# Output and branch steps of the second tile's mixers in two parts each, with two slots of the expert sum behind each part

## The chip, the cores and the metric

One Trainium2 chip, one of its NeuronCores. The program is one launch. The metric is the device time of the launch in microseconds (us); lower is better. The engines are TensorE (PE), VectorE (DVE), ScalarE (ACT), GpSimd (POOL) and SyncE (SP); each works through its own list of instructions in order and waits for the others by semaphores. SP and POOL issue the transfers (DMA) from the chip's memory.

## The reference, cut to what matters

256 tokens of width 1024 in float32 go through two blocks. The first block has two mixers (a gated delta rule, and the HGRN2 recurrence), a mix of the two branches, and a retrieval of experts; the second block has pooling, attention and two feed-forward layers. The change lies in the first block:

```
o_b = _hgrn2_recurrence(...)            # chunks of 64 tokens: o = q S + a v ;  S = S * f + k v
y_a = o_a @ w_branch_a ; y_b = o_b @ w_branch_b
mix = sigmoid(g_a) * y_a + sigmoid(g_b) * y_b
x = x + mix @ w_out
h2 = rmsnorm(x) ; idx, gate = two top-16 searches over (h2 @ w_pq) and sub_keys
x = x + sum over 128 chosen experts of gate * gelu(h2 . expert_u[idx]) * expert_v[idx]
```

## The kernel before

The tokens are two tiles of 128. Each tile goes through the mixers (`delta0`, `hgrn0` for the first tile, `delta1`, `hgrn1` for the second), then through its tile steps (`tile0`, `tile1`), and then through the sum over its 128 chosen experts. The sum of the first tile is spread over the mixers and tile steps of the second tile, whose results it doesn't need.

**One slot of the expert sum.** A slot `r` (0 to 127 for the first tile, 128 to 255 for the second) is one expert for each of 128 tokens: one indirect transfer by POOL (line 888) gathers 128 rows of 8 KB, so 1 MB. DVE makes the dot product of half of each row with `h2` (line 906, with `accum_out`). ACT turns the dots of two slots (an even and the following odd one) into weights (lines 941, 944) and, except where `r` is a multiple of 4, writes the weight as a diagonal matrix (line 953). PE multiplies that diagonal with the other half of the row, into a sum in PSUM (line 972, two halves of 512 columns, which the trace shows as four rows per slot). Every fourth slot is added by DVE instead (line 919). The sum or add of slot `r` stands three slots behind its dot (`BEHIND = 3`): where the order table says that the slots up to `r` are worked on, PE sums slots up to `r - 3`.

**Buffers and gathers.** `Experts.place` decides beforehand which of 17 buffers a slot gets. POOL issues the gathers strictly in the order of the slots, and each waits until the slot that used the buffer before has been summed or added. Slot 71 takes the buffer of slot 63, slot 142 that of slot 128. From slot 72 on (`PARTS_FROM = 72`) the gathers wait for `hgrn_done(1)`, the last instruction of the second tile's HGRN mixer (line 793), because two of the buffers are its inputs. Four buffers are the places of the streamed weight panels, free for gathers only for slots 12 to 55 and from 128 on.

**Weight panels.** Weights stream in panels of 2 MB through two places; SP issues a panel when PE has finished the product that used its place (`stream`, line 360). The panels of the second tile are two for each of `branch_a`, `branch_b` and `w_out`, and four for `w_pq`. The product of a tile with one panel is 8 matmuls of 512 columns (`product_of_tile`, line 469).

**The order table.** `mixers_order` writes one list of entries `(program, stop)`. Each engine has one generator for each program, and `walk` runs the list on each engine: it advances the named generator up to the named `yield`. Entries made by `rows(n)` advance the expert sum by `n` slots. So an entry that has no instruction of an engine costs that engine nothing, and the table alone decides what stands before what in an engine's list.

The steps of `hgrn1` that the change touches, for each chunk `ch` of 64 tokens: PE makes the output `o.ch` (8 pairs of matmuls, lines 1484 and 1485) and the new part of the state `s.ch` (line 1443); DVE scales the state (line 1424, after `o.ch`) and adds `s.ch` (line 1426); ACT copies `o.ch` out (line 1362). `o.1` reads the state that DVE has made from `s.0`. After both chunks the gated norm follows (lines 774 to 793), whose last instruction is `hgrn_done`.

The steps of `tile1`: `turn_a`, `turn_b` turn the two mixers' outputs; `a`, `b` are the products with `branch_a` and `branch_b` (DVE multiplies each half by its gate, line 1696); `mix` adds and turns; `out` is the product with `w_out` (DVE adds to x, line 1709); `norm` makes `h2` and turns it; then the projections (`pq`), the scores (line 1590) and the searches `top`, `best`, `name` of five groups, nearly all of it DVE work.

## Time and profile before

| | us |
|---|---|
| median of 3 runs | 2010.41 (2004.6 to 2016.08) |
| the profiled execution, own time | 2016.91 |
| its span, first to last instruction | 2015.1 |

| engine | busy us | share |
|---|---|---|
| PE | 1728.3 | 86% |
| DVE | 821.7 | 41% |
| ACT | 449.5 | 22% |
| POOL | 310.8 | 15% |

In the profile, a row of a timeline gives the start in us from the span's start, the length in us, engine, line, operation, what it writes and reads, how many instructions are merged in it, and in brackets how long the engine had been idle before and what released it. A row of the windows gives, for one stretch, the busy us of PE, PE's weight loads, DVE, ACT and POOL (with counts of instructions), then the granted clock of TensorE (1.00 is 2.4 GHz, 0.50 is 1.2 GHz), the busy share of the DMA engines, and GB/s. A row of the DMA view gives a queue's packets, megabytes and share; the queue `q0` carries the gathers of POOL, `q1` what SP issues.

### The profile page before, as it was taken

What the parts mean: (1) busy time and instruction counts of PE and PEld (TensorE: products, weight loads), DVE (VectorE), ACT (ScalarE), POOL (GpSimd) and SP (SyncE); (2) the same over time, 40 slices, a digit from 0 to 9 for tenths busy, and PEclk for the clock granted to TensorE, in tenths of its full rate; (3) what the DMA queues carried; (4) which work ended last, traced back from release to release, by engine and by line L of the source; (5) the groups of instructions that cost most, each with busy time, mean ns of one, the idle gap of its engine ahead of it and who ended that gap; (6) DMA issues with size and microseconds to landing.
All of it is one profiled execution on the core that took longest, in us unless ns stands there. A gap on an engine that the chain in (4) does not pass through costs nothing.

```text
span 2015.1 us, 17726 instructions
## 1 busy us (share of the span) xinstructions
PE 1728.3 (86%) x6952; PEld 1135.5 (56%) x6952; DVE 821.7 (41%) x1564; ACT 449.5 (22%) x990; POOL 310.8 (15%) x260
## 2 busy tenths in 40 slices
PE   7999988997898588788965875677999999799998
PEld 6857656773675355434622422226887476478853
DVE  2433124422267786535999766662000013410001
ACT  1142114221132344212333322222000012310000
POOL 0000000000002253223344554430000000000000
PEclk9999978998889788789987989889999999899999
DMA  6444211114368799699999999993444343153442
GB/s 228 153 167 167 84 42 42 53 73 177 146 237 343 306 373 422 272 425 423 419 421 382 421 421 422 422 422 153 167 167 149 143 177 137 42 188 134 159 167 105
DMA packets 55184, 471.14 MB, mean 234 GB/s; under 512 B 6592, under 2 KB 7744, under 8 KB 10432
## 3 DMA queue, kind: packets, MB, share of 16 engines
q0 software_dynamic: 36864, 268.45, 32.4%
q1 hardware_dynamic: 18240, 201.60, 26.7%
q8 instruction: 53, 0.87, 0.2%
q14 instruction: 27, 0.22, 0.0%
HBM read 468.98 MB, written 1.05 MB: 233 GB/s over the span
## 4 chain that ended last, share of the span: by engine, by line
PE 61%; DMA 15%; DVE 14%; ACT 4%; issue 3%; POOL 1%; POOLq 0%; DVEq 0%; SPq 0%; ACTq 0%
PE ps L2282 15%; DMA main<-in_expert_uv,main 8%; PE ps L2306 7%; PE ps L469 6%; PE ps L425 6%; DMA panels<-in_expert_uv,main 5%; PE ps L395 4%; PE ps L1211 4%; DVE main L906 4%; PE ps L972 3%; PE ps L2259 3%; PE ps L2263 2%; PE ps L1443 2%; DMA panels<-in_wall 2%; PE ps L465 2%
## 5 line engine op out<-in xcount | busy, mean ns | idle before, releaser
L888 POOL DMA_INDIRECT main<-in_expert_uv,main x200 | 242.1, 1211 | 949.1 <-DVE main L1777 556.8
L972 PE MATMUL ps<-main 128*128 128x512 f32 x596 | 305.6, 663 | 81.5 <-ACT main L953 79.0
L2282 PE MATMUL ps<-xT,panels 128*128 128x256 f32 x1408 | 304.5, 379 | 0.8 <-DMA panels<-in_wall 0.8
L2282 PEld LDWEIGHTS ps<-xT,panels 128*128 128x128 f32 x1408 | 267.3, 190 | 37.2 <-DMA panels<-in_wall 0.9
L906 DVE SCALAR_TENSOR_TENSOR main<-main 128x1024 f32<-128x1024 f32 x200 | 240.7, 1223 | 106.5 <-DMA main<-in_expert_uv,main 105.0
L972 PEld LDWEIGHTS ps<-main 128*128 128x128 f32 x596 | 121.5, 213 | 246.8 <-issue 133.5
L2306 PE MATMUL ps<-panels,main 128*128 128x512 f32 x352 | 151.9, 593 | 2.3 <-DMA panels<-in_wall 2.3
L2359 DVE TENSOR_TENSOR main<-main,ps 128x512 f32<-128x512 f32 x22 | 15.1, 688 | 288.4 <-PE ps L2282 250.4
L972 PE MATMUL ps<-panels,main 128*128 128x512 f32 x172 | 93.7, 691 | 45.2 <-ACT main L953 38.4
L941 ACT ACTIVATE main<-main 128x2 f32<-128x2 f32 x128 | 25.9, 203 | 440.3 <-DVE main L906 334.7
L425 PE MATMUL ps<-panels,xT 128*128 128x512 f32 x256 | 117.0, 611 | 1.4 <-DVE main L1193 1.4
L2306 PEld LDWEIGHTS ps<-panels,main 128*128 128x128 f32 x352 | 66.7, 190 | 86.4 <-issue 82.3
L1211 PEld LDWEIGHTS ps<-main 128*128 128x128 f32 (+1 forms) x704 | 86.4, 200 | 14.8 <-issue 10.3
L1211 PE MATMUL ps<-main 128*128 128x128 f32 (+1 forms) x704 | 88.6, 284 | 5.8 <-ACT main L1087 1.7
L972 PEld LDWEIGHTS ps<-panels,main 128*128 128x128 f32 x172 | 36.4, 223 | 98.1 <-issue 61.1
L469 PE MATMUL ps<-panels,main 128*128 128x512 f32 x192 | 87.6, 616 | 3.4 <-ACT main L527 2.3
L395 PE MATMUL ps<-xT,panels 128*128 128x256 f32 x384 | 85.3, 386 | 1.3 <-PEq L562 1.3
L425 PEld LDWEIGHTS ps<-panels,xT 128*128 128x128 f32 x256 | 48.9, 196 | 58.1 <-issue 56.4
L395 PEld LDWEIGHTS ps<-xT,panels 128*128 128x128 f32 x384 | 74.4, 194 | 12.1 <-issue 1.7
L888 POOL DMA_INDIRECT panels<-in_expert_uv,main x56 | 68.5, 1223 | 81.2 <-DVE xT L919 27.2
L1443 PE MATMUL ps<-main 128*128 128x128 f32 (+1 forms) x288 | 50.3, 346 | 35.5 <-DVE main L1402 32.0
L906 DVE SCALAR_TENSOR_TENSOR panels<-panels,main 128x1024 f32<-128x1024 f32 x56 | 67.7, 1224 | 28.1 <-DMA panels<-in_expert_uv,main 27.6
(270 smaller groups left out, 1913.2 us busy)
## 6 DMA issues: line engine op xcount, KB each, us to landing
panels<-in_wall SPq DMA_DIRECT2D x88, 2048.0 KB, 8.0
main<-in_rows SPq DMA_DIRECT2D x14, 512.0 KB, 6.8
main<-in_expert_uv,main POOLq DMA_INDIRECT x200, 18.1
main<-in_sub_keys SPq DMA_DIRECT2D x2, 1024.0 KB, 13.9
mats<-in_mats SPq DMA_DIRECT2D x1, 1088.0 KB, 5.4
x<-in_x SPq DMA_DIRECT2D x2, 512.0 KB, 3.9
main<-in_pool_w SPq DMA_DIRECT2D x1, 1024.0 KB, 33.6
main<-in_rel_bias SPq DMA_DIRECT2D x1, 1024.0 KB, 15.1
```

What stands on the lines that cost most here:

```text
L395: mm = pe.matmul(self.ps[:, bank, t * T:(t + 1) * T], w[:, k, c:c + P], actT[:, k, :], start=(k == 0), stop=(k == KC - 1))
L425: mm = pe.matmul(self.ps[:, bank, :], self.xT[:, k, j * P:(j + 1) * P], w[:, k, :], start=(k == 0), stop=(k == KC - 1))
L465: mm = pe.matmul(self.ps[:, bank, t * P:(t + 1) * P], w[:, k, t * P:(t + 1) * P], actT[:, k, :], start=(k == 0), stop=(k == KC - 1))
L469: mm = pe.matmul(self.ps[:, bank, :], actT[:, k, :], w[:, k, :], start=(k == 0), stop=(k == KC - 1))
L888: pool.indirect_dma_start(out=self.bufs[self.buf_of[r]], out_offset=None, in_=self.c.dram["expert_uv"], in_offset=bass.IndirectOffsetOnAxi ...
L906: dve.scalar_tensor_tensor(out=u, in0=u, scalar=1.0, in1=self.c.row(m, H2), op0=ALU.mult, op1=ALU.mult, accum_out=self.dots_at[:, m, q:q + ...
L972: mm = pe.matmul(self.c.ps[:, b, :], self.diags[self.of_pe(r) % DIAG_RING], v[:, half * HALF:(half + 1) * HALF], start=(q == 1), stop=(q = ...
L1211: mm = pe.matmul(out[:, h, :], lhs(h), rhs(h), start=True, stop=True)
L1443: mm = pe.matmul(out[:, h, :], lhs(h), rhs(h), start=True, stop=True)
L2259: mm = pe.matmul(c.ps[:, bank, t * T + m * P:t * T + (m + 1) * P], w[:, k, at:at + P], c.xT[:, k, m * P:(m + 1) * P], start=(k == 0), stop ...
L2282: mm = pe.matmul(c.ps[:, bank, t * T:(t + 1) * T], w[:, k, at:at + P], c.xT[:, k, :], start=(k == 0), stop=(k == KC - 1))
L2306: mm = pe.matmul(c.ps[:, 4 + 2 * m + half, :], hidden[:, n, m * P:(m + 1) * P], w[:, n % 4, half * HALF:(half + 1) * HALF], start=(n == 0) ...
```

## The change

Two kinds of entries of the table are cut in two. In `hgrn1` the new stop `seen{ch}` stands behind the matmuls of `o.ch` and before those of `s.ch` (on DVE and ACT it stands before everything of the chunk); two slots follow it, and two, then one, follow the stops `o{ch}` and `S{ch}`. In `tile1` the steps `a`, `b` and `out` have a stop behind the product with their first panel (`a0`, `b0`, `out0`), and two slots follow each of the seven stops. No instruction is added or taken away; the slots after both chunks stand at 72 where they stood at 70, and the two extra slots are taken back at the end of the first tile's sum, behind `best3`.

```diff
@@ hgrn_tensor
         mm.then_inc(un.filled(), 1)
+        yield f"seen{ch}"
         heads(f"s.{ch}", lambda h: t.k_dec[r, h, :], lambda h: t.v[r, h, :])
@@ tile_tensor
-    c.products_of_tile(pe, t.names[0], t.aT, channel_major=False)
+    c.product_of_tile(pe, t.names[0], 0, t.aT, channel_major=False)
+    yield "a0"
+    c.product_of_tile(pe, t.names[0], 1, t.aT, channel_major=False)
     yield "a"
@@ tile_vector
             dve.tensor_tensor(at, at, c.ps[:, bank, :], ALU.mult).then_inc(c.bank_read[bank].sem, 1)
+            if q == 0:
+                yield ("a0", "b0")[n]
@@ mixers_order
     for ch in range(2):
+        part("hgrn1", f"seen{ch}")
+        rows(2)
         part("hgrn1", f"o{ch}")
-        rows(3)
+        rows(2)
         part("hgrn1", f"S{ch}")
         rows(1)
...
-    part("tile1", "a")
-    rows(4)
...
-    part("tile1", "out")
-    rows(4)
+    for x in ("a0", "a", "b0", "b", "mix", "out0", "out"):
+        part("tile1", x)
+        rows(2)
     part("tile1", "norm")
     rows(3)
```

The same stops stand in the ACT programs and for `b0` and `out0`. How the lists of the engines move is seen best in the lists themselves. First PE, before, around the second chunk of `hgrn1`: L1443 x8 is `s.0` and later `s.1`, the pairs of L1484 and L1485 between are `o.1`, and L972 with x6 is the sum of three slots.

```order
L1443 MATMUL ps<-main 128x128 x8
L972 MATMUL ps<-main 128x512 x6
L1484 MATMUL ps<-main 128x128
L1485 MATMUL ps<-main 128x128
...
L1443 MATMUL ps<-main 128x128 x8
L972 MATMUL ps<-main 128x512 x10
L518 MATMUL ps<-mats,main 128x128 x8
```

The same place of the PE list in the changed kernel (its lines 1445, 1486 and 1487 are the same instructions):

```order
L972 MATMUL ps<-main 128x512 x2
L1445 MATMUL ps<-main 128x128 x8
L972 MATMUL ps<-main 128x512 x6
L1486 MATMUL ps<-main 128x128
L1487 MATMUL ps<-main 128x128
...
L972 MATMUL ps<-main 128x512 x2
L1445 MATMUL ps<-main 128x128 x8
L972 MATMUL ps<-main 128x512 x10
L518 MATMUL ps<-mats,main 128x128 x8
```

Slot 59 is now summed before `s.0`, slots 61, 62 and 63 before `o.1` (before: 59, 61, 62), and slot 65 between `o.1` and `s.1`.

Next DVE, before, from the first chunk's state (L1424, L1426) to the gated norm (L786); L906 is a dot, L919 an add:

```order
L906 SCALAR_TENSOR_TENSOR main<-main 128x1024
L1424 TENSOR_TENSOR main<-main 128x1024
L1426 TENSOR_TENSOR main<-main,ps 128x1024
L906 SCALAR_TENSOR_TENSOR main<-main 128x1024 x3
L919 SCALAR_TENSOR_TENSOR xT<-main,xT 128x8x128
L906 SCALAR_TENSOR_TENSOR main<-main 128x1024
L1424 TENSOR_TENSOR main<-main 128x1024
L1426 TENSOR_TENSOR main<-main,ps 128x1024
L906 SCALAR_TENSOR_TENSOR main<-main 128x1024
L786 TENSOR_REDUCE small<-main 128x8
```

And in the changed kernel, where L1426 and L1428 are the two state instructions:

```order
L906 SCALAR_TENSOR_TENSOR main<-main 128x1024 x2
L1426 TENSOR_TENSOR main<-main 128x1024
L1428 TENSOR_TENSOR main<-main,ps 128x1024
L906 SCALAR_TENSOR_TENSOR main<-main 128x1024 x2
L919 SCALAR_TENSOR_TENSOR xT<-main,xT 128x8x128
L906 SCALAR_TENSOR_TENSOR main<-main 128x1024 x3
L1426 TENSOR_TENSOR main<-main 128x1024
L1428 TENSOR_TENSOR main<-main,ps 128x1024
L906 SCALAR_TENSOR_TENSOR main<-main 128x1024
L919 SCALAR_TENSOR_TENSOR xT<-main,xT 128x8x128
L786 TENSOR_REDUCE small<-main 128x8
```

The dot of slot 65 now stands before the first state step, those of slots 69 and 70 before the second one, and the dot of slot 71 and the add of slot 68 before the norm.

Last PE again, the tile steps, before; L469 is a product, 8 for each panel, and L518 a turn:

```order
L469 MATMUL ps<-panels,main 128x512 x16
L972 MATMUL ps<-main 128x512 x6
L469 MATMUL ps<-panels,main 128x512 x16
L972 MATMUL ps<-main 128x512 x6
L518 MATMUL ps<-mats,main 128x128 x8
L972 MATMUL ps<-main 128x512 x4
L469 MATMUL ps<-panels,main 128x512 x16
```

and in the changed kernel:

```order
L469 MATMUL ps<-panels,main 128x512 x8
L972 MATMUL ps<-main 128x512 x2
L469 MATMUL ps<-panels,main 128x512 x8
L972 MATMUL ps<-main 128x512 x4
L469 MATMUL ps<-panels,main 128x512 x8
L972 MATMUL ps<-main 128x512 x2
L469 MATMUL ps<-panels,main 128x512 x8
L972 MATMUL ps<-main 128x512 x4
L518 MATMUL ps<-mats,main 128x128 x8
L972 MATMUL ps<-main 128x512 x2
L469 MATMUL ps<-panels,main 128x512 x8
```

The sums of one or two slots stand between the products with the two panels of each weight.

## Rows read from the trace of the kernel before

**Rows 1.** The page: span, and GB/s in 40 equal slices of 50.4 us.

```profile
span 2015.1 us, 17726 instructions
...
GB/s 228 153 167 167 84 42 42 53 73 177 146 237 343 306 373 422 272 425 423 419 421 382 421 421 422 422 422 153 167 167 149 143 177 137 42 188 134 159 167 105
```

**Rows 2.** Windows: busy us of each engine, clock, DMA share, GB/s.

```profile
core 0: us, PE busy (x) PEld busy (x) DVE busy (x) ACT busy (x) POOL busy (x), PEclk, DMA share, GB/s
855.00:1070.00 215.00, 165.15 (x576) 90.15 (x576) 153.62 (x417) 58.40 (x163) 73.87 (x63) 0.89 1.01 422
1070.00:1085.00 15.00, 10.84 (x19) 4.70 (x20) 14.90 (x26) 5.88 (x19) 6.14 (x5) 0.68 0.83 311
1085.00:1366.00 281.00, 196.91 (x398) 79.61 (x396) 184.56 (x277) 78.70 (x277) 139.51 (x109) 0.90 1.00 416
...
828.00:845.00 17.00, 17.00 (x51) 10.43 (x51) 9.40 (x11) 5.83 (x9) 1.21 (x2) 0.73 0.18 65
```

**Rows 3.** Timeline of POOL: the gathers of slots 71, 72 and 142.

```profile
837.99 0.94 POOL L888 DMA_INDIRECT main<-in_expert_uv,main  x1 [17.82 <-PE ps L972]
844.73 1.68 POOL L888 DMA_INDIRECT main<-in_expert_uv,main  x1 [5.80 <-DVE main L793]
...
1074.72 1.68 POOL L888 DMA_INDIRECT panels<-in_expert_uv,main  x1 [13.83 <-DVE xT L916]
```

**Rows 4.** Timeline of PE, 800 to 845 us.

```profile
800.99 0.46 PE L1484 MATMUL ps<-main 128*128 128x128 f32 x2
...
807.53 1.95 PE L1443 MATMUL ps<-main 64*128 64x128 f32 x16
...
815.48 2.60 PE L972 MATMUL ps<-main 128*128 128x512 f32 x4 [2.36 <-ACT main L953]
819.33 0.80 PE L1484 MATMUL ps<-main 128*128 128x128 f32 x2 [1.26 <-DVE main L1426]
...
830.77 3.62 PE L1443 MATMUL ps<-main 64*128 64x128 f32 x16
834.32 10.26 PE L972 MATMUL ps<-main 128*128 128x512 f32 x20
```

**Rows 5.** Timeline of DVE, 813 to 845 us: dots of slots 63 and 67, state, norm.

```profile
813.14 1.23 DVE L906 SCALAR_TENSOR_TENSOR main<-main 128x1024 f32<-128x1024 f32 x1 [5.54 <-DMA main<-in_expert_uv,main]
...
818.05 1.22 DVE L1426 TENSOR_TENSOR main<-main,ps 128x1024 f32<-128x1024 f32 x1
...
823.07 1.23 DVE L906 SCALAR_TENSOR_TENSOR main<-main 128x1024 f32<-128x1024 f32 x1 [1.22 <-DMA main<-in_expert_uv,main]
...
839.15 1.22 DVE L786 TENSOR_REDUCE small<-main 128x8 f32<-128x1024 f32 x1 [2.16 <-ACT main L774]
...
843.23 1.22 DVE L793 TENSOR_TENSOR main<-main,small 128x1024 f32<-128x1024 f32 x1
```

**Rows 6.** Timeline of PE from the start of the `branch_a` product.

```profile
873.61 13.97 PE L469 MATMUL ps<-panels,main 128*128 128x512 f32 x32 [1.56 <-ACT main L527]
887.42 5.31 PE L972 MATMUL ps<-main 128*128 128x512 f32 x12
```

**Rows 7.** Timeline of DVE: slots 79, 99, first search, slots 111 and 128.

```profile
870.41 1.22 DVE L906 SCALAR_TENSOR_TENSOR main<-main 128x1024 f32<-128x1024 f32 x1 [1.25 <-DMA main<-in_expert_uv,main]
...
951.94 1.23 DVE L906 SCALAR_TENSOR_TENSOR main<-main 128x1024 f32<-128x1024 f32 x1 [1.25 <-DMA main<-in_expert_uv,main]
...
960.22 0.48 DVE L1726 MAX8 main<-main 128x8 f32<-128x128 f32 x2
...
995.23 1.22 DVE L906 SCALAR_TENSOR_TENSOR main<-main 128x1024 f32<-128x1024 f32 x1
...
1069.12 1.22 DVE L906 SCALAR_TENSOR_TENSOR panels<-panels,main 128x1024 f32<-128x1024 f32 x1
```

**Rows 8.** DMA queues, 0 to 951.9 us: packets, MB, share.

```profile
q0 software_dynamic: 14498, 105.66, 27.4%
```

**Rows 9.** DMA queues, 0 to 1000 us: packets, MB, share.

```profile
q0 software_dynamic: 16514, 120.32, 29.7%
```

More of the change, by code:

```diff
@@ L1421, in hgrn_vector @@
         last = CHUNK * (ch + 1) - 1
+        yield f"seen{ch}"
         yield f"o{ch}"
@@ L1486, in hgrn_tensor @@
         mm.then_inc(un.filled(), 1)
+        yield f"seen{ch}"
         heads(f"s.{ch}", lambda h: t.k_dec[r, h, :], lambda h: t.v[r, h, :])
@@ L1545, in tile_tensor @@
         pe.wait_ge(c.bank_read[b].sem, n)
-    c.products_of_tile(pe, t.names[1], t.bT, channel_major=False)
+    c.product_of_tile(pe, t.names[1], 0, t.bT, channel_major=False)
+    yield "b0"
+    c.product_of_tile(pe, t.names[1], 1, t.bT, channel_major=False)
     c.uses_at[f"mix.{m}"] = list(c.bank_uses)
@@ L1552, in tile_tensor @@
     wait_turned_tile_read(c, pe)
-    c.products_of_tile(pe, t.names[2], t.mixT, channel_major=False)
+    c.product_of_tile(pe, t.names[2], 0, t.mixT, channel_major=False)
+    yield "out0"
+    c.product_of_tile(pe, t.names[2], 1, t.mixT, channel_major=False)
     c.uses_at[f"out.{m}"] = list(c.bank_uses)
@@ L1624, in tile_scalar @@
     read_turned_tile(c, act, t.bT, 4 * m + 1)
-    yield "a"
-    yield "b"
+    for stop in ("a0", "a", "b0", "b"):
+        yield stop
     read_turned_tile(c, act, t.mixT, 4 * m + 2)
-    yield "mix"
-    yield "out"
+    for stop in ("mix", "out0", "out"):
+        yield stop
     for b in (0, 2):
@@ L1709, in tile_vector @@
         dve.tensor_tensor(at, at, c.ps[:, bank, :], ALU.add).then_inc(c.bank_read[bank].sem, 1)
+        if q == 0:
+            yield "out0"
     yield "out"
@@ L1967, in mixers_order @@
     rows(4)
-    part("tile1", "a")
-    rows(4)
-    part("tile1", "b")
-    rows(4)
-    part("tile1", "mix")
-    rows(2)
-    part("tile1", "out")
-    rows(4)
+    for x in ("a0", "a", "b0", "b", "mix", "out0", "out"):
+        part("tile1", x)
+        rows(2)
     part("tile1", "norm")
```

## The prediction, on record before the changed kernel ran

> **What bounds the kernel now.** I first read the page's row of GB/s [rows 1]: from slice 12 to slice 26 (605 to 1360 us) the gathers fill the memory path at about 422 GB/s, with holes in slices 13, 14, 16 and 21. The change acts from 807 us on, so only the holes of slices 16 and 21 are in question. The windows cut them out [rows 2]: from 828 to 845 us the DMA share is 0.18, which is 14 us lost; from 855 to 1070 it is 1.01, nothing lost; from 1070 to 1085 it is 0.83, 2.6 us lost; from 1085 to 1366 it is 1.00. What follows after 1366 doesn't depend on the order in question. So the time moves by what the gathers' stream moves: when it resumes near 845, and how long it runs dry near 1075.
>
> The timeline of POOL names the gates [rows 3]. Slot 71's gather waited 17.8 us for a sum on PE and went out at 837.99: it needs slot 63's buffer, and that sum stood behind `o.1` and `s.1`. Slot 72's waited for line 793, `hgrn_done(1)`, and went out at 844.73. Slot 142's went out at 1074.72, after the first DVE instruction for slot 128 (line 916), which stands behind the last search of `tile1`. In 855 to 1070 DVE is the other full engine: from the first search at 960.22 to slot 128's dot at 1069.12 [rows 7] it has next to no idle time.
>
> **The first hole, piece by piece.** In the changed kernel slot 63's sum stands before `o.1`, so slot 71's gather leaves at about 821 instead of 837.99. That is the full 17 us that the move seems to promise, but it buys one gather: slot 72 and all behind it still wait for `hgrn_done(1)`. So I follow that chain, from the rows of PE and DVE [rows 4, 5].
>
> - Up to 813 nothing arrives earlier: slot 63's dot starts at 813.14 when its row lands, and its weight lets PE sum slots 62 and 63 from 815.48. The first takes 2.60 us as now, the second 1.8 to 3.5. PE is free at 820 to 821.6.
> - DVE now makes slot 65's dot before the first state step. Rows land about every 2.5 us here (1 MB at 422 GB/s), slot 67's at 823.07, so slot 65's at 818.1. The dot (1.2) and two state instructions (2.45) give 821.8. Now the state is ready at 819.27 (818.05 + 1.22). **`o.1` starts at 821.9, 2.6 us later than now.**
> - `o.1` took 11.4 us (819.33 to 830.77), while `o.0`, the same 8 pairs of matmuls, took 6.5 (800.99 to 807.53). The granted clock explains it: 1.2 GHz for the one, 2.4 for the other. PE had idled 2.36 and 1.26 us just before the slow one. In the change two 512-column sums stand together right before `o.1`, with about 1 us of idle time left. The row at 834.32 shows what such sums do: five slots took 10.26 us, near the 1.77 for a slot at full clock [rows 6], so the clock had come back under them after `s.1`. I take the full clock for `o.1`, and keep the other.
> - With the full clock: `o.1` ends 828.4, slot 65's sum 830.2, `s.1` 832.1. DVE meanwhile waits for rows: slots 69 and 70 land at 828.0 and 830.5, the dot of 70 ends at 831.7, two state instructions end at 834.2. Slot 71's row has landed (833), its dot ends 835.4, the add of slot 68 836.6; ACT's weight and square put the norm's reduction at 837.7. From there to the end of line 793 it is 5.3 us (839.15 to 844.45): 843.0. **The resume moves by -1.5 us.** It can't be much better whatever PE does: slots 70 and 71 have to land first.
> - With the half clock: `o.1` ends 833.3, the sum by 836.8, `s.1` at 838.7 to 840.4; state, dot, add, weight and square add 5 us, the norm 5.3: 849.0 to 850.7, **+4.5 to +6.2**.
>
> **The tile steps.** Two more slots stand before `a`. PE started it at 873.61, released by ACT, which had waited for slot 79's dot at 870.41 [rows 6, 7]. Now it is slot 81's, two rows later: the products start 5.0 us later against the stream. From there on the counts are alike: 14 slots up to `norm` before and after, on PE 10 sums where there were 11. The interleaving lets ACT weigh one pair less before the turned mix can be read, and two dots less stand before the square of x; each saves 1 to 3 us of waiting, and three sums instead of two before the projections give 1.8 back. So the path from `a` to the first search, 86.6 us now (873.61 to 960.22), gets back most of the 5.0 us. The rows themselves are there: slot 99's dot ran at 951.94 as soon as its row landed, slot 101's runs two rows later, at 956.9, and ends at 958.1. I let the search start 1 to 2 us earlier than now, and that matters little, as the next part shows: what is late on PE here is covered by the wait for rows there, up to some 6 us. The last panel loads of `w_pq` and what SP issues behind them start about 5 us later too.
>
> **The second hole.** From the first search on DVE has the same work less two dots: 28 slots up to 128 before, 26 after, 2 x 1.2 = 2.4 us. But it asks for rows two numbers higher at the same place, with no stock: slot 99 was still waited for at 951.94. The queue view says when a row is there [rows 8, 9]: at 951.9 us 105.66 MB had come for slots 0 to 99 (104.86 MB), so 0.8 MB lies in rows behind; slot 113 (114 rows, 119.54 MB) is in when 120.34 MB have come, at 1000.0 us. DVE took slot 111 at 995.23 before, and would take slot 113 at that place, by its own work at about 993.3. So it waits for the stream. The loads of SP that came in between (`w_pq`, then the pooling constants) begin about 5 us later and leave the gathers a little more of the path; I take 1.0 us from it. Slot 113's dot then ends at 1000.2. Slot 111's ended at 996.4 and slot 128's began 72.7 us later; less 2.4 that is 70.3, so 1070.5, **+1.4 us** against 1069.12 (0 to +2.8 by how SP's loads fall). As the stream runs dry there now, slot 142's gather, and everything behind, moves by it. If DVE were not starved, the hole would close: -2.6 us, no more, since the share is 1.0 on both sides.
>
> **A rule that speaks against it.** The granted clock in 828 to 845 is 0.73 with PE busy throughout [rows 2, 4]. The Trainium skill, "TensorE: Matmul & The Clock Gate", section "A second HAM failure mode: psum-queue depth-cycling", says that short idle gaps between groups of matmuls can make the clock swing and that the groups then pay for it. By that rule finer pieces on PE hold the clock down; this trace agrees in so far as short gaps stood before the slow `o.1`. Its result here is the first rival below.
>
> **Sum.** -1.5 + 1.4 = -0.1 us against the profiled execution's 2016.9, which lies 6.5 above the median of the runs shown; I take the difference over to the median: 2010.3.
>
> **The rivals.**
> 1. *The forecast*: full clock in `o.1`, DVE starved a little: -0.1 (-1.5 to +1.3). Chance 0.50.
> 2. *Slower: the clock stays at 1.2 GHz* through `o.1`, slot 65's sum and `s.1`, as now through `o.1`. For it: the gaps before `o.1` shrink but don't go. Against it: the sums just ahead. 4.5 + 1.4 = +5.9, up to 6.2 + 2.8 = +9.0, so 2016.3 to 2019.4. It passes the bound of 0.5% (10 us) only where `hgrn_done` comes 8.5 us later than 844.45 or the runs' own spread adds to it. Chance 0.25.
> 3. *Both edits pay*: resume -1.5 and the hole near 1075 gone, -4.1, so 2006.3. For it: DVE has 2.4 us less to do and starts searching earlier. Against it: the byte count above. Chance 0.18.
> 4. *The 14 us hole closes*, -10 or more. The wait on line 793 excludes it unless the norm comes much earlier, and the landing of slot 71 excludes that. Chance 0.03. The rest, 0.04, is for panels of `branch_b` landing later beside a deeper queue of gathers (12.3 us are free for each, a panel product and three sums [rows 6]).
>
> The runs of the kernel before spread from 2004.6 to 2016.1, so a difference under 0.5% is about what a measurement of this kernel can't tell from none. The range takes cases 1 to 3 and a little of that spread: 2003 to 2020. Faster by over 0.5%: 0.03 and a part of case 3, 0.07. Slower by over 0.5%: a part of case 2 and the panels, 0.13. Within: 0.80.
>
> **What the profile of the changed kernel would show.** Slot 71's gather within 2 us of slot 70's, and the long idle time of POOL before the gather of slot 72, still released by line 793, at 843 (or 849 to 851 if rival 2 is right). The windows still with a hole of some 12 to 18 us before it. The second run of lines 1486 and 1487 in 6.5 us at clock 1.0, starting near 822. `branch_a`'s product near 877, with sums between its panels and no wait for panels. DVE waiting for gathers at slots 105 to 113, which it doesn't now, and a hole near 1075 of 2 to 6 us. The prediction is wrong if the gather of slot 72 is released by something else, if DVE never waits in its searches, or if the part after 1366 changes in length.

## The result, and the profile after

The changed kernel took 2015.26 us in the median of 20 runs (2007.41 to 2023.78), the kernel before 2007.15 us in 20 runs beside it (2001.69 to 2016.08). The ratio is 1.0035 with an interval of 1.002 to 1.005: slower by 7 us (4 to 10), where -0.1 was forecast. The profiled execution of the changed kernel took 2013.05 us.

The two profiled executions already differ by 8 us ahead of slot 63's dot (it starts at 813.14 before [rows 5], at 805.18 after), in a part whose code is the same. So from here on times within the stretch count from **the start of slot 63's dot**, written t+. First the page and the windows of the changed kernel, to be laid beside [rows 1, 2]:

```profile
span 2011.3 us, 17726 instructions
...
GB/s 228 155 165 170 84 42 43 64 63 178 146 274 344 281 401 423 268 423 424 419 421 386 421 421 422 422 415 132 172 163 155 138 181 133 42 189 135 158 167 105
```

```profile
core 0: us, PE busy (x) PEld busy (x) DVE busy (x) ACT busy (x) POOL busy (x), PEclk, DMA share, GB/s
821.00:839.00 18.00, 17.66 (x56) 9.21 (x55) 11.28 (x15) 7.09 (x14) 0.00 (x0) 0.84 0.14 56
855.00:1070.00 215.00, 164.13 (x575) 89.04 (x574) 155.96 (x422) 59.95 (x167) 70.67 (x60) 0.87 1.01 418
1070.00:1085.00 15.00, 14.57 (x31) 5.86 (x31) 14.90 (x22) 5.42 (x21) 10.00 (x9) 0.92 0.88 353
1085.00:1366.00 281.00, 194.51 (x393) 78.38 (x392) 183.11 (x273) 77.76 (x273) 134.93 (x106) 0.89 0.98 408
```

Slice 16 still has its hole (268 GB/s, before 272), and the first window has a share of 0.14 over 18 us: 15.5 us lost, where it was 14. POOL's timeline, beside [rows 3], says why:

```profile
812.49 0.94 POOL L888 DMA_INDIRECT main<-in_expert_uv,main  x1 [0.30 <-issue]
839.50 0.94 POOL L888 DMA_INDIRECT main<-in_expert_uv,main  x1 [26.07 <-DVE main L793]
...
1070.23 1.68 POOL L888 DMA_INDIRECT panels<-in_expert_uv,main  x1 [22.11 <-DVE xT L916]
```

Slot 71's gather goes out at once after slot 70's (t+7.3, before t+24.9). Slot 72's waits for line 793 as before, and goes out at t+34.3 instead of t+31.6. Slot 142's is at t+265.1 instead of t+261.6. PE in the second chunk of `hgrn1`, beside [rows 4]:

```profile
807.51 3.70 PE L972 MATMUL ps<-main 128*128 128x512 f32 x8 [1.69 <-ACT main L953]
813.81 0.49 PE L1486 MATMUL ps<-main 128*128 128x128 f32 x2 [2.60 <-DVE main L1428]
...
815.90 0.48 PE L1487 MATMUL ps<-main 64*128 64x128 f32 x2
816.31 0.68 PE L1486 MATMUL ps<-main 128*128 128x128 f32 x2
816.92 0.79 PE L1487 MATMUL ps<-main 64*128 64x128 f32 x2
...
823.43 3.60 PE L972 MATMUL ps<-main 128*128 128x512 f32 x4
826.96 2.05 PE L1445 MATMUL ps<-main 64*128 64x128 f32 x16
```

`o.1` begins at full clock (0.49 us for two matmuls). From 816.9 on the same two take 0.79: the granted clock has fallen to 1.2 GHz. It stays there through slot 65's sum (3.60 us for what takes 1.8 to 2 at full clock) and is back at `s.1`. PE had stood idle for 1.69 and 2.60 us just before. The norm, beside [rows 5], ends 2.8 us later against slot 63 than it did (t+34.1 against t+31.3):

```profile
829.11 1.22 DVE L1428 TENSOR_TENSOR main<-main,ps 128x1024 f32<-128x1024 f32 x1 [4.18 <-PE ps L1445]
...
833.92 1.22 DVE L786 TENSOR_REDUCE small<-main 128x8 f32<-128x1024 f32 x1 [1.12 <-ACT main L774]
...
838.00 1.23 DVE L793 TENSOR_TENSOR main<-main,small 128x1024 f32<-128x1024 f32 x1
```

And DVE further on, the waits that stand beside [rows 7]:

```profile
921.53 0.69 DVE L1720 TENSOR_TENSOR x<-x,ps 128x512 f32<-128x512 f32 x1 [5.91 <-PE ps L469]
...
931.83 0.69 DVE L1720 TENSOR_TENSOR x<-x,ps 128x512 f32<-128x512 f32 x1 [7.32 <-PE ps L469]
...
954.64 0.49 DVE L1739 MAX8 main<-main 128x8 f32<-128x128 f32 x2 [1.74 <-ACT main L1664]
961.01 1.28 DVE L919 SCALAR_TENSOR_TENSOR xT<-main,xT 128x1024 f32<-128x1024 f32 x1 [0.65 <-ACT main L944]
986.46 1.23 DVE L906 SCALAR_TENSOR_TENSOR main<-main 128x1024 f32<-128x1024 f32 x1 [2.48 <-DMA main<-in_expert_uv,main]
```

The products start at t+68.0 (PE's first matmul with `branch_a`), before at t+60.5. DVE waits 5.91 and 7.32 us for the two halves of the `w_out` product. The kernel before has this pair of waits too:

```profile
923.22 0.69 DVE L1709 TENSOR_TENSOR x<-x,ps 128x512 f32<-128x512 f32 x1 [6.50 <-PE ps L469]
930.09 0.69 DVE L1709 TENSOR_TENSOR x<-x,ps 128x512 f32<-128x512 f32 x1 [6.18 <-PE ps L469]
```

The first search starts at t+149.5, before at t+147.1. Slot 111's dot waits 2.48 us for its row in the midst of the searches, where nothing waited before. From slot 142's gather to slot 255's it is 264.5 us; before it is 265.7. So in the profiles the stream behind slot 142 is shifted, not stretched, and what is to be explained lies ahead of it.

### The profile page after: what moved, and what is told of

The parts are those of the page before. It is cut to its first block, busy times and chain, and to the rows that moved or that the text cites. A ratio compares the mean times of both kernels' runs of the same rounds, so it can differ in the third digit from the quotient of the medians.

```text
span 2011.3 us, 17726 instructions
## 1 busy us (share of the span) xinstructions
PE 1715.6 (85%) x6952; PEld 1122.6 (56%) x6952; DVE 822.1 (41%) x1564; ACT 449.4 (22%) x990; POOL 309.4 (15%) x260
## 4 chain that ended last, share of the span: by engine, by line
PE 61%; DMA 16%; DVE 13%; ACT 4%; issue 3%; POOL 2%; POOLq 0%; DVEq 0%; SPq 0%; ACTq 0%
PE ps L2292 15%; DMA main<-in_expert_uv,main 10%; PE ps L2316 7%; PE ps L469 6%; PE ps L425 6%; DMA panels<-in_expert_uv,main 5%; PE ps L395 4%; PE ps L1211 4%; PE ps L972 4%; DVE main L906 3%; PE ps L2269 3%; PE ps L2273 2%; PE ps L1445 2%; PE ps L465 2%; DMA panels<-in_wall 2%
## 5 line engine op out<-in xcount | busy, mean ns | idle before, releaser
L972 PE MATMUL ps<-main 128*128 128x512 f32 x596 | 309.3, 667 | 89.4 <-ACT main L953 88.9
L906 DVE SCALAR_TENSOR_TENSOR main<-main 128x1024 f32<-128x1024 f32 x200 | 241.0, 1222 | 114.6 <-DMA main<-in_expert_uv,main 110.5
L972 PEld LDWEIGHTS ps<-main 128*128 128x128 f32 x596 | 121.4, 214 | 256.0 <-issue 135.2
L972 PE MATMUL ps<-panels,main 128*128 128x512 f32 x172 | 90.2, 669 | 52.9 <-ACT main L953 46.2
L972 PEld LDWEIGHTS ps<-panels,main 128*128 128x128 f32 x172 | 35.0, 214 | 103.9 <-issue 69.2
L469 PE MATMUL ps<-panels,main 128*128 128x512 f32 x192 | 87.9, 615 | 4.5 <-ACT main L527 3.2
L906 DVE SCALAR_TENSOR_TENSOR panels<-panels,main 128x1024 f32<-128x1024 f32 x56 | 67.6, 1222 | 28.1 <-DMA panels<-in_expert_uv,main 25.1
```

The source lines that it names most:

```text
L469: mm = pe.matmul(self.ps[:, bank, :], actT[:, k, :], w[:, k, :], start=(k == 0), stop=(k == KC - 1))
L906: dve.scalar_tensor_tensor(out=u, in0=u, scalar=1.0, in1=self.c.row(m, H2), op0=ALU.mult, op1=ALU.mult, accum_out=self.dots_at[:, m, q:q + ...
L972: mm = pe.matmul(self.c.ps[:, b, :], self.diags[self.of_pe(r) % DIAG_RING], v[:, half * HALF:(half + 1) * HALF], start=(q == 1), stop=(q = ...
```

## The experiments

Each was timed in five rounds beside the kernel before, 12 runs in all (6 for e15, 7 for e17); the first two rows have the times of the section above. "hd" is the end of the last line 793 (`hgrn_done`), "g" a gather's issue, "d" a dot's start. All of these are read from one profiled execution of each and counted from slot 63's dot. The length of `o.1` is taken from the start of its first row to that of its last. "Slots" says how many slots stand before the tile's products and before the first search.

| kernel | slots | ratio, interval | o.1, us | hd | g72 | products | d128 | g142 |
|---|---|---|---|---|---|---|---|---|
| before | 80/100 | 1 | 10.8 | 31.3 | 31.6 | 60.5 | 256.0 | 261.6 |
| changed | 82/102 | 1.0035, 1.002 to 1.005 | 8.9 | 34.1 | 34.3 | 68.0 | 259.5 | 265.1 |
| e1 | 82/102 | 1.0016, 0.9999 to 1.0033 | 9.5 | 36.6 | 36.9 | 71.3 | 265.2 | 270.8 |
| e2 | 80/100 | 0.999, 0.9974 to 1.0006 | 10.9 | 31.3 | 31.5 | 60.5 | 256.4 | 262.0 |
| e3 | 80/100 | 1.0003, 0.9985 to 1.002 | 10.1 | 32.9 | 33.1 | 61.6 | 258.8 | 264.4 |
| e4 | 80/100 | 0.9959, 0.994 to 0.9977 | 9.4 | 30.5 | 25.6 | 55.1 | 251.6 | 257.2 |
| e5 | 82/102 | 1.002, 0.9995 to 1.0045 | 6.2 | 30.9 | 31.2 | 65.9 | 259.4 | 265.0 |
| e6 | 80/100 | 1.0008, 0.9984 to 1.0031 | 9.8 | 33.1 | 33.3 | 62.1 | 259.6 | 265.1 |
| e7 | 82/102 | 0.9976, 0.9952 to 1.0 | 6.2 | 30.0 | 12.6 | 50.9 | 245.1 | 250.7 |
| e8 | 80/100 | 0.9983, 0.9958 to 1.0009 | 10.8 | 27.9 | 28.2 | 57.0 | 252.6 | 258.2 |
| e9 | 82/100 | 1.003, 1.0007 to 1.0052 | 6.1 | 30.9 | 31.1 | 63.5 | 258.4 | 264.0 |
| e10 | 80/100 | 0.998, 0.9957 to 1.0004 | 9.6 | 30.0 | 30.3 | 58.4 | 243.6 | 253.5 |
| e11 | 82/102 | 0.9945, 0.9925 to 0.9964 | 10.9 | 37.6 | 13.7 | 59.0 | 241.3 | 251.2 |
| e12 | 80/100 | 0.9988, 0.997 to 1.0006 | 9.3 | 30.4 | 24.8 | 54.6 | 241.0 | 250.9 |
| e13 | 80/100 | 0.9987, 0.9972 to 1.0001 | 6.1 | 29.0 | 29.3 | 58.6 | 254.1 | 259.8 |
| e14 | 80/102 | 1.0034, 1.0014 to 1.0054 | 6.3 | 29.9 | 30.1 | 58.6 | 256.8 | 262.4 |
| e15 | 82/102 | 0.9933, 0.9914 to 0.9951 | 6.3 | 30.0 | 12.6 | 51.4 | 233.5 | 243.4 |
| e16 | 80/100 | 0.9998, 0.998 to 1.0015 | 6.1 | 25.2 | 25.5 | 53.9 | 249.5 | 255.1 |
| e17 | 80/100 | 0.9965, 0.9946 to 0.9984 | 6.2 | 28.5 | 17.9 | 50.4 | 237.5 | 247.4 |

**Which half of the change.** Both edits are made on the changed kernel: e1 gives it the tile steps of before, e2 the `hgrn1` steps of before.

```diff
-    for x in ("a0", "a", "b0", "b", "mix", "out0", "out"):
-        part("tile1", x)
-        rows(2)
+    part("tile1", "a")
+    rows(4)
+    part("tile1", "b")
+    rows(4)
+    part("tile1", "mix")
+    rows(2)
+    part("tile1", "out")
+    rows(4)
```

```diff
-        part("hgrn1", f"seen{ch}")
-        rows(2)
         part("hgrn1", f"o{ch}")
-        rows(2)
+        rows(3)
```

> Only the half of the change in hgrn1 (seen, o, S followed by 2, 2 and 1 slots per chunk); the tile steps keep 4, 4, 2 and 4 slots. Theory A (the loss is that hgrn_done, and with it the gather of slot 72, comes later): all of the loss is here, +4 to +8 us against before, ratio 1.002 to 1.004, and the gather of slot 72 comes 32 to 35 us after the dot of slot 63, where it came 31.6 us after it before. Theory B (the loss comes from the sums between the halves of the products and the wait for rows in the searches behind them): 0 to +1 us. The forecast on record: -0.1 us.

> Only the half of the change in tile1 (two slots behind each of a0, a, b0, b, mix, out0, out); hgrn1 keeps 3 and 1 slots per chunk. Theory A: 0 us or a little faster (-3 to +1), since the slots before the products stand where they stood and the path to the first search is 1 to 3 us shorter. Theory B: +4 to +8 us. The forecast on record would give -1 to -3 us, down to the 2.6 us of the second hole.

e2 can't be told from before in its time, and its columns lie within 0.5 us of it: parting the tile steps alone brings nothing. In its profile e1 has the whole shift and more: `o.1` mostly at half clock, `hgrn_done` 5.3 us later, slot 128 9.2 us later. Its time, 1.0016, is clear neither of before nor of the changed kernel. So it is the profiles that put the loss in the edit in `hgrn1`; the times show that the tile edit alone doesn't have it.

**The slots or the stops.** e3 is the changed kernel with one slot behind `o{ch}` instead of two, so that the counts are those of before:

```diff
         part("hgrn1", f"o{ch}")
-        rows(2)
+        rows(1)
```

> The whole change with one slot instead of two behind o0 and o1, so that 4 slots stand in each chunk as before, and slot 71 is no longer dotted before the norm. Theory A, if the loss is the work put before the norm (the wait for the row of one more slot, its dot, an add): hgrn_done comes 1 to 4 us earlier than in the full change and the ratio falls to 0.999 to 1.002. Theory A, if the loss is the granted clock in o.1 alone: no gain against the full change, 1.003. Theory B: 1.003 as well, as the tile steps keep their form.

Ratio 1.0003, with `hgrn_done` 1.6 us and slot 128 2.8 us later than before: between the two in the profile, and no loss in the time that can be measured.

**The price of a late gate.** e6 is the kernel before with four more DVE instructions, 5.00 us in its trace, ahead of the second tile's gated norm (they write a buffer that nothing reads any more); e8 is the kernel before with the four slots behind `o1`, `S1` all behind the gate step; e4 moves the gate itself, so that the gathers need the HGRN buffers only from slot 84 on, and e7 is the same on the changed kernel. The edits, in this order:

```diff
+    if m == 1:
+        for _ in range(4):
+            step(dve.tensor_tensor(t.k_t, t.k_t, t.k_t, ALU.mult))
```

```diff
-    for ch in range(2):
-        part("hgrn1", f"o{ch}")
-        rows(3)
-        part("hgrn1", f"S{ch}")
-        rows(1)
-    part("hgrn1", "gate")
+    part("hgrn1", "o0")
+    rows(3)
+    part("hgrn1", "S0")
+    rows(1)
+    part("hgrn1", "o1", "S1", "gate")
+    rows(4)
```

```diff
-PARTS_FROM = 72
+PARTS_FROM = 84
```

> The kernel before with four more DVE multiplications of 1.2 us, one after the other, before the reduction of hgrn1's norm (on a slot of memory that nobody reads any more). A dose for theory A: hgrn_done comes 4.9 us later, slot 72's gather 36.5 us after slot 63's dot instead of 31.6, and if the stream of gathers sets the end the time rises by 4 to 5 us, ratio 1.0020 to 1.0025; slot 142's gather moves by as much. If the later hole or DVE takes it up: 0 to 1 us.

> The kernel before with the four slots of the second chunk of hgrn1 moved behind the norm, so that o.1, s.1, the state and the norm follow each other without a dot between. Theory A: slot 72's gather is released earlier, by 1 to 3 us (one dot less and no weights before the square), but slot 71's may be later; ratio 0.998 to 1.000. If only the granted clock counts: 1.000.

> The kernel before with PARTS_FROM 84 instead of 72: the two buffers that lie in the inputs of the HGRN mixer take their first slot at 84, and no gather before slot 84 waits for hgrn_done. Theory A (the wait of slot 72 for hgrn_done opens the hole of 14 us, and the stream of gathers sets the end): the hole shrinks by 5 to 12 us and the time falls by 2.6 us to 12 us, as far as DVE follows (the second hole near 1075 takes the rest): ratio 0.994 to 0.999. Theory B: the end hangs on DVE's searches, and these on the products; the products start on slot 79's dot, so they start earlier too; 0.995 to 1.0. If the hole costs nothing: 1.000.

> The changed kernel with PARTS_FROM 84 instead of 72, so that no gather before slot 84 waits for hgrn_done. If the loss of the change is the later hgrn_done, it is gone here: the sums of slots 63 to 67 stand early, the gathers from 72 on leave 18 to 27 us after slot 63's dot, and the time is 5 to 12 us under before and at or under that of the same edit on the kernel before (0.9959): ratio 0.993 to 0.997. If the change costs time elsewhere (product stage, searches), it stays 3 to 6 us above that one: 0.998 to 1.0.

Slot 72's gather 3.4 us earlier (e8) brings slot 142's 3.4 earlier; 6.0 (e4) brings 4.4; 21.7, from the changed kernel to e7, brings 14.4. e6 was a weaker dose than meant: DVE had stood idle for 2.16 us ahead of the norm [rows 5], and `o.1` was 1.0 us shorter in that execution, so `hgrn_done` came only 1.8 later, yet slot 142's gather 3.5. So in these pairs two thirds or more of what slot 72's gather gains or loses is handed on to slot 142; e5 below is an exception. e4 is also clearly faster in time, and e7, with all of the change in it, has 0.9976 where the changed kernel has 1.0035. But e7's expectation missed: its time isn't under e4's 0.9959 (the intervals overlap), though its profile has slot 142's gather 6.5 us earlier. e7's POOL timeline around slot 72:

```profile
814.19 0.94 POOL L888 DMA_INDIRECT main<-in_expert_uv,main  x1 [0.99 <-PE ps L972]
818.82 1.82 POOL L888 DMA_INDIRECT main<-in_expert_uv,main  x1 [3.70 <-DVE xT L919]
823.76 1.85 POOL L888 DMA_INDIRECT main<-in_expert_uv,main  x1 [3.12 <-PE ps L972]
827.65 1.62 POOL L888 DMA_INDIRECT main<-in_expert_uv,main  x1 [2.04 <-PE ps L972]
```

Each gather waits a few us for a buffer, none for line 793. Slice 16 of its page is at 394 GB/s.

**The clock.** e5 is the changed kernel with three matmuls that nothing reads, put where PE waits for the state ahead of `o.1`:

```diff
+        if m == 1 and ch == 0:
+            for _ in range(3):
+                pe.matmul(c.ps[:, 0, :], c.mat("ident"), c.mats[:, 0:4, :].rearrange("p h n -> p (h n)"),
+                          start=True, stop=True)
```

> The changed kernel with three more matmuls on PE between slot 63's sum and the wait for the state before o.1 (a constant matrix into a bank that nothing reads; they write no result). They fill some 2.6 us in which PE waits for DVE anyway. Clock theory (the norm is late because TensorE's granted clock falls within o.1 after that wait): o.1 runs in about 6.5 us instead of 9.6, slot 72's gather comes 28 to 31 us after slot 63's dot instead of 34.3, and the time falls by 3 to 6 us against the changed kernel, ratio to before 0.998 to 1.001. Work theory (the dots and adds that stand before the norm make it late, whatever the clock): slot 72's gather stays at 33 to 35 us, ratio 1.002 to 1.004.

```profile
808.87 5.40 PE L972 MATMUL ps<-main 128*128 128x512 f32 x8 [1.99 <-ACT main L953]
814.10 2.74 PE L1495 MATMUL ps<-mats 128*128 128x512 f32 x6
...
822.83 0.48 PE L1487 MATMUL ps<-main 64*128 64x128 f32 x2
823.24 1.98 PE L972 MATMUL ps<-main 128*128 128x512 f32 x4
```

With the idle time filled, `o.1` takes 6.2 us at full clock to its last pair, slot 65's sum 1.98. `hgrn_done` comes 3.2 us earlier than in the changed kernel, though the filler itself makes `o.1` start 1.5 us later. The seven kernels with the filler all have 6.1 to 6.3 us; of the twelve without, e7 alone has. e1 and e7 have the same lists up to there, and rows that agree to 0.02 us: 5.40 us of sums, idle times of about 1.97 and 0.91 us. Yet in e1 (first three rows) the clock fell within `o.1`, and slot 65's sum took 3.78; in e7 (last three) it stayed and the sum took 1.98:

```profile
808.36 5.40 PE L972 MATMUL ps<-main 128*128 128x512 f32 x8 [1.96 <-ACT main L953]
814.67 0.49 PE L1486 MATMUL ps<-main 128*128 128x128 f32 x2 [0.91 <-DVE main L1428]
...
824.92 3.78 PE L972 MATMUL ps<-main 128*128 128x512 f32 x4
...
808.52 5.40 PE L972 MATMUL ps<-main 128*128 128x512 f32 x8 [1.98 <-ACT main L953]
814.84 0.49 PE L1486 MATMUL ps<-main 128*128 128x128 f32 x2 [0.92 <-DVE main L1428]
...
821.50 1.98 PE L972 MATMUL ps<-main 128*128 128x512 f32 x4
```

e11 has the same order up to there too and took 10.9 us at clock 0.50, where PE had been idle for 3.65 us just before. Its row, and then e7's window, 6.2 us at 1.00:

```profile
809.57 0.80 PE L1486 MATMUL ps<-main 128*128 128x128 f32 x2 [3.65 <-DVE main L1428]
```

```profile
814.80:821.00 6.20, 6.16 (x30) 4.44 (x30) 4.89 (x7) 1.27 (x5) 2.14 (x2) 1.00 1.02 422
```

So without the filler the clock there is a chance of the execution, and the idle time alone doesn't decide it. That the filler keeps it up, seven profiles of seven show; they show it in the profile alone, since e5's time (1.002) can't be told from the changed kernel's. But e5 moves slot 128 by 0.1 us alone: a second loss stands behind the first.

**The second loss.** Its candidates are the two slots more ahead of the products and the two more ahead of the first search. e9, e13 and e14 complete four corners around e5, all with the filler. In order e9, e13, e14, against e5:

```diff
     part("tile1", "norm")
-    rows(3)
+    rows(1)
```

```diff
         part("hgrn1", f"o{ch}")
-        rows(2)
+        rows(1)
```

```diff
     part("hgrn1", "gate")
-    rows(3)
+    rows(1)
...
     part("tile1", "norm")
-    rows(3)
+    rows(5)
```

> The changed kernel with the three filling matmuls before o.1, and with one slot instead of three behind tile1's norm, so that 100 slots stand before the first search, as before the change, and not 102. Two-cause theory (the change costs once through o.1 at a low clock, which the filling takes away, and once through two more rows that DVE asks for in its searches before the stream has them): slot 128's dot comes 255 to 257 us after slot 63's, where it came 256.0 before, 259.5 in the changed kernel and 259.4 with the filling alone, and the time is that of before, ratio 0.999 to 1.001. One-cause theory (only the late hgrn_done): no gain against the run with the filling alone, slot 128's dot at 259 to 260, ratio 1.002.

> The changed kernel with three identity matmuls of 512 columns ahead of the second tile's output chunk 1 (they write a row block that nothing reads any more, so that TensorE has no idle time before that chunk), and with one slot instead of two behind each of the two new output parts: 80 slots before the tile's products and 100 before the first search, as in the kernel before. Theory (the 3 us that stay when the clock is filled away come from the two slots that stand ahead of the products and the two that stand ahead of the search): slot 128's dot at 255.5 to 256.5 us after slot 63's (before: 256.0; with the filler and all slots: 259.4), slot 142's gather at 261 to 262, products at 59 to 61, ratio 0.998 to 1.001. Rival (the parts themselves, or the three fillers, cost it, whatever the slots): slot 128's dot again at 258.5 to 259.5, ratio 1.001 to 1.004.

> The same filler, one slot behind the gate step and five behind the norm step: 80 slots before the products, and 102 before the first search, as in the changed kernel. Theory A (the later products carry the loss): slot 128's dot at 255.5 to 257 us after slot 63's, products at 59 to 61, ratio 0.998 to 1.001. Theory B (the two slots more before the search carry it, since the searches then ask for rows two numbers higher while the gathers are no further on): slot 128's dot at 258.5 to 259.5 and DVE waiting for rows at slots 107 to 113, ratio 1.001 to 1.004. In between (257 to 258.5): each carries a part.

| d128 after slot 63's dot, ratio | 100 before the search | 102 |
|---|---|---|
| 80 before the products | 254.1, 0.9987 | 256.8, 1.0034 |
| 82 before the products | 258.4, 1.003 | 259.4, 1.002 |

In the profiles each step adds something: 4.3 and 2.6 us for the slots before the products, 2.7 and 1.0 for those before the search. But each is one profile, and the corners aren't clean. e5, e9 and e14 have the same lists up to `hgrn_done` and still lie 1.0 us apart there, and e13 ends it up to 1.9 us earlier, since it takes its slots out ahead of the norm. So the 1.0 isn't clear of the scatter, and of the 4.3 up to 1.9 is an earlier gate. In time e9 and e14 are slower than before; e13 isn't, and e5's interval takes in 1.

Where the second loss lies is seen at the start of the first search. In e5 the late products have been made good by then: it starts at t+146.0, before at t+147.1. The wait of 7.33 us for the second `w_out` product is no new loss, as the pair of waits there is 13.24 us, and 12.68 in the kernel before. From the first search to slot 128's dot it is 108.9 us before, 108.9 in e9 and 109.0 in e13, all with 100 slots ahead of it; with 102 and so two dots less to make, it is 110.0 in the changed kernel, 112.8 in e14 and 113.4 in e5. DVE's rows in e5:

```profile
920.79 0.69 DVE L1724 TENSOR_TENSOR x<-x,ps 128x512 f32<-128x512 f32 x1 [5.91 <-PE ps L469]
...
931.09 0.69 DVE L1724 TENSOR_TENSOR x<-x,ps 128x512 f32<-128x512 f32 x1 [7.33 <-PE ps L469]
...
983.45 1.22 DVE L906 SCALAR_TENSOR_TENSOR main<-main 128x1024 f32<-128x1024 f32 x1 [2.18 <-DMA main<-in_expert_uv,main]
987.72 1.22 DVE L906 SCALAR_TENSOR_TENSOR main<-main 128x1024 f32<-128x1024 f32 x1 [3.04 <-DMA main<-in_expert_uv,main]
```

So the second loss is the wait for rows in the searches: 0.49, 2.18 and 3.04 us at slots 107, 110 and 111, where before has none. In e9 these are gone, and this one stands ahead of the first search:

```profile
962.31 1.28 DVE L919 SCALAR_TENSOR_TENSOR xT<-main,xT 128x1024 f32<-128x1024 f32 x1 [8.52 <-ACT main L944]
```

The add needs a weight that ACT makes only after it has copied out the scores. The kernel before has that wait too (5.84 us); with 102 slots the weight is made earlier and 0.65 is left. So e9's expectation missed: taking back the two slots cures the rows and brings this wait back, longer by 2.7 us, and the search starts at t+149.5. e14 has row waits of 1.48 and 3.48 us in the searches, and e13 none there. e14's time (1.0034) is worse than its profile (+0.8 us at slot 142); one profile of each kernel can't settle that.

**The filler in the kernel before.** e16 adds the lines of e5 to the kernel before, and nothing else.

> The kernel before with the same three identity matmuls of 512 columns ahead of the second tile's output chunk 1, and nothing else: it has one order step less to wait through there, and its chunk 1 took 10.8 us at half the clock. Theory (the half clock in chunk 1 is a loss that the kernel before has as well, and the parts bring nothing of their own): chunk 1 in 6.1 to 6.5 us, the tile's last state write at 28 to 29.5 us after slot 63's dot (before: 31.3), slot 128's dot at 253 to 254.5 (before: 256.0; the changed kernel with four slots less in front and the filler, e13: 254.1), ratio 0.9975 to 1.0. Rival (e13's 254.1 is owed to the parts, and the filler only pays back what the parts cost): the last state write at 30 to 31.5, slot 128's dot at 255.5 to 257, ratio 0.999 to 1.002.

`o.1` takes 6.1 us, `hgrn_done` comes 6.1 us earlier and slot 142's gather 6.5, more than was expected. e13 has the same slot counts and the same filler, with the new stops besides: it ends `hgrn_done` 3.8 us behind e16 and starts slot 128's dot 4.6 us behind it. So at one and the same clock the change makes `hgrn_done` later by itself: 3.8 us in e13, 5.7 in e5. In its profile the kernel before paid for a slow `o.1`, and that had hidden this. Yet e16's time is 0.9998, so what the profile gains isn't seen in it. In this execution the tail from slot 255's dot to the end took 657.1 us, and 649.7 in that of before; over all the profiles it is 650 to 657, with the same code.

**A better version.** e10 gives the steps of the last search (group 4; two expectations call it the fourth) two slots each in the kernel before. The table had `rows(3)` there, nine slots by its text, but `most` is 128 and slot 128 had been reached ahead of this search, so no slot stood in it; now slots 128 to 133 do. Further, e11 puts that and the gate at 84 on the changed kernel, e12 on the kernel before; e15 adds the filler to e11, and e17 has e3's slot counts besides.

```diff
-        part("tile1", f"top{g}")
-        rows(3)
-        part("tile1", f"best{g}")
-        rows(3)
-        part("tile1", f"name{g}")
-        rows(3)
+        n, most = (2, SLOTS + 8) if g == 4 else (3, SLOTS)
+        for x in ("top", "best", "name"):
+            part("tile1", f"{x}{g}")
+            rows(n, most)
```

> The kernel before with two slots behind each step of the last search (top4, best4, name4) where it had none, and so slots 128 to 133 begun before the search is over. If the hole of 2.6 us near 1075 comes from slot 142's gather waiting for slot 128's first add, that gather leaves some 10 us earlier, the hole closes and the time falls by 2 to 3 us: ratio 0.9985 to 0.999. If the hole is opened by something else: 1.000.

> The changed kernel with both holes attacked: PARTS_FROM 84, and two slots behind each step of the last search. The stream of gathers should have less than 3 us of idle time from slot 63 to slot 255. Against before (14 us and 2.6 us of holes, one gather of 2.5 us in them) that is -13 to -17 us in the stream: ratio 0.992 to 0.995. If DVE is the bound of that stretch instead, slot 255's dot gains no more than with PARTS_FROM 84 alone (11 us), ratio 0.996 to 0.998.

> The same two edits on the kernel before (PARTS_FROM 84, and two slots behind each step of the last search), so without the change. Against the run with both edits on the changed kernel it shows what the change is worth once slot 72 no longer waits for the norm: there slots 63 and 65 are summed ahead of s.1, here the stream waits for them behind o.1 and s.1 (7 to 9 us of idle time in the first hole). Expected ratio 0.994 to 0.997; if the change costs time in the tile steps, this one is the faster of the two.

> The changed kernel with the parts' products from slot 84 instead of 72, the fourth search's steps on six slots instead of nine, and the filler. Theory (the clock lost in output chunk 1 is the delay of the gated gather that e11 kept): output chunk 1 in 6.2 us instead of 10.9, the second tile's last state write at 30 to 31 us after slot 63's dot instead of 37.6, slot 142's gather at 245 to 249 instead of 251.2, slot 255's at 514 to 517 instead of 519.4, ratio 0.990 to 0.994. Rival (the stream's bytes to slot 142 and the fourth search decide, not the gate): slot 142's gather stays at 250 to 252, ratio 0.9935 to 0.996.

> e15 (parts' products from slot 84, the fourth search's steps on six slots, the filler) with one slot instead of two behind each output part, so 80 slots before the products and 100 before the first search. Theory (the two slots in front cost 2 to 5 us at slot 128 in the kernels with a gated gather at 72, as e13 against e5 and e14 shows): slot 142's gather 2 to 4 us earlier than e15's 243.4, ratio 0.990 to 0.993. Rival (with the gate moved to slot 84 the rows are far enough ahead that the searches don't starve DVE): slot 142's gather at 242.5 to 244.5, ratio 0.992 to 0.995, the same as e15 (0.9933 [0.9914, 0.9951]).

e15 is the fastest: 1996.37 us against 2008.26, ratio 0.9933 (0.9914 to 0.9951). It had 6 runs. Its windows, with both holes all but closed:

```profile
801.00:856.00 55.00, 45.13 (x146) 22.87 (x144) 39.84 (x55) 17.53 (x50) 23.16 (x21) 0.94 0.99 405
1036.00:1051.00 15.00, 4.93 (x7) 1.80 (x8) 14.62 (x53) 5.15 (x12) 1.03 (x2) 0.61 0.92 380
```

Beside e11 the profile has 7.8 us less at slot 142, the time only 0.9933 against 0.9945, which their intervals don't part. e12 against e11 went the other way than their profiles: slot 142's gather at 250.9 and 251.2, but ratios 0.9988 and 0.9945. That stays open, and e12 missed its expectation (0.994 to 0.997). e10 brings slot 142's gather 8.1 us forward, but slot 255's only 3.6 (t+523.7 against t+527.3), and its interval takes in 1. e17's theory fell, and slot 142's gather came even later than its rival had it: in this pair of profiles the two slots in front no longer cost; without them DVE waits 6.94 us for the same add as in e9, and the gather is 4.0 us later.

## Why the prediction was wrong

**Right.** The move buys slot 71's gather alone: it left at t+7.3 (forecast 7.9), and slot 72's went on waiting for line 793. `o.1` starts at t+8.6 (forecast 8.8, before 6.2). Where the clock was full the rest of that sum holds: e5 and e7 end line 793 at t+30.9 and t+30.0, against a forecast of 29.9. The products start 5.4 us later against the stream in e5 (forecast 5.0), and the path from them to the first search gives back 5.1 us in the changed kernel (68.0 to 149.5 is 81.5, before 86.6). The first search starts 1.1 us earlier than before in e5 (forecast 1 to 2). DVE waits for rows in the searches. In the profiles the part behind slot 142 keeps its length.

**The step that failed** is "two 512-column sums stand together right before `o.1`, with about 1 us of idle time left ... I take the full clock for `o.1`". It was drawn from the row at 834.32 [rows 4], where five slots of sums ran with no gap. That row has no group behind it that waits for a state, so it doesn't bear the step. In the changed kernel the two sums ran in 3.70 us, faster than taken (2.60 and 1.8 to 3.5), PE was left idle for 2.60 us, and the clock fell within `o.1`: 3.1 us were lost there and 1.8 in slot 65's sum, and the term of -1.5 us measured +2.8. Nor was the length of the idle time the fault, since in e1 it was 0.91 us, about what was forecast, and the clock fell all the same; in e7, with the same 0.92, it stayed. Two sums ahead of `o.1` leave the clock open.

The gain of 1.5 us was a gain of clock alone. It set a slow `o.1` before against a fast one after. With a fast one in both, `hgrn_done` is at t+25.2 before (e16) and at t+30.9 or 30.0 after (e5, e7), 4.8 to 5.7 us later. What differs in the lists is the work that now stands ahead of the two state steps and the norm, the dots of slots 65, 69, 70 and 71 and the add of slot 68. The forecast had it right, at t+29.9, but set it against a kernel before at half clock. The second rival had the mechanism; its 4.5 to 6.2 for this term is what e1 (+5.3) and e11 (+6.3) show, with the clock at half for longer, and the changed kernel lies between. The Trainium skill, "TensorE: Matmul & The Clock Gate", section "A second HAM failure mode: psum-queue depth-cycling", tells of a bf16 kernel in which short idle gaps between groups of matmuls make the clock swing, at the cost of throughput. By that rule the changed kernel's trace agrees (gaps of 1.69 and 2.60 us, then the fall), and the seven profiles with the filler, which closes the second gap (to 0.86 us in e17), don't speak against it; e7, with gaps of 1.98 and 0.92 us and no fall, doesn't. I had weighed this rival at one in four.

**The term that was too small** is the second hole, +1.4 us with bounds of 0 to +2.8. With the clock filled away (e5) it is +3.4 at slot 128, beyond the upper bound. The kind was right: DVE asks for rows two numbers higher at the same place and finds no stock. The size wasn't. I had checked one slot, 113, by the bytes that had come, and put its dot at t+185.9; in e5 DVE waits 5.7 us in all at 107, 110 and 111, and the dot of 113 starts at t+188.9 (t+189.0 in the changed kernel). From there to slot 128 it is 70.5 us, forecast 71.5. Why the rows of 110 and 111 land so late stays open.

**The sum.** At slot 142 the profile has +3.5 us, which isn't -1.5 + 1.4, nor 2.8 + 3.4 either, since the waits for rows grow as the gate comes earlier (2.48 us in the searches of the changed kernel, 5.7 in e5): e5 takes 3.1 us off slot 72's gather and 0.1 off slot 142's. The time has +7 (4 to 10). The median itself, 2015.26 us, lies within the forecast's 2003 to 2020; that range was as wide as the spread of single runs, and 20 runs of each tell less than half a per cent. The other 3.5 us I can't place: each kernel has one profile, and the granted clock differs between executions. Over the kernels the two do go together: in all 19, time against slot 255's gather has a slope of 0.76 us per us and a correlation of 0.80, with up to 5.4 us beside the line.

**The rivals.** The third (both edits pay) fell with the changed kernel's rows, a later resume and DVE waiting in its searches, and in e2 the tile parts alone bring nothing. The fourth (the 14 us hole closes) needs another gate, as was said, and e7 shows that it is there to be had: 14.4 us at slot 142.

## What to carry to other kernels

Where gathers go out strictly in order, ask what the first one behind the hole waits for: an edit that frees the one ahead of it buys one transfer. Moving that gate by twelve slots (one constant) was worth 0.4 to 0.6%, more than any other single edit here. And don't count on the clock of a group of matmuls that follows an idle time: of twelve profiles here without a filler one kept it, and spare matmuls in the wait kept it in seven of seven. Set the forecast against the kernel before at the same clock, or a gain of clock hides what the order costs. When a table moves slots past a step, look at both ends: fewer slots ahead of the searches brought a wait of 5.8 to 8.5 us for ACT, more brought waits for rows.

## What the runs showed of the hardware

- The same rows can be followed by either clock: e1 and e7 agree to 0.02 us up to `o.1`, with idle times of about 1.97 and 0.91 us, and then `o.1` ran at a mean granted clock of 0.59 in e1 and 1.00 in e7. In e11 `o.1` ran all its 11.6 us at 0.50 after an idle time of 3.65 us; of the 512-column sums behind it slot 65's took 3.78 us and the next ones 1.8 each. With three spare matmuls of 2.74 us in all ahead of it, `o.1` ran at 1.00 in all seven profiles.
- The run-to-run spread of one kernel goes with the clock granted over the whole run: over 145 runs of the kernel before, 1.35 us less per 0.001 of mean clock, correlation -0.79, with clocks from 0.922 to 0.936. The spread of these runs, 1999.45 to 2025.86 us, is larger than the effect of this change (7 us), so single runs can't show it.
